# Conditioning columns from 2048 on as VectorE sums in a two-layer diffusion backbone

## What is computed

```python
silu_c = jax.nn.silu(c)
silu_cc = jax.nn.silu(c_ctx)
for l in range(DEPTH):
    mod_x = silu_c @ w_ada[l] + b_ada[l]      # 1024 x 6144 weights
    mod_c = silu_cc @ w_ada[l] + b_ada[l]
    sh1, sc1, g1, sh2, sc2, g2 = jnp.split(mod_x[:, None, :], 6, axis=-1)
    ...
    hx = _rmsnorm(x, norm1[l]) * (1.0 + sc1) + sh1
    ox, oc = _mixer(...)            # projection to 2304 columns, three kinds of heads, output projection
    x = x + g1 * ox
    hx2 = _rmsnorm(x, norm2[l]) * (1.0 + sc2) + sh2
    x = x + g2 * _ec_moe(hx2, ...)  # 16 experts, each takes its 64 best latents
    ...                             # the same for the context, in layer 0 only
return _rmsnorm(x, norm_final)
```

## Time and profile before

| | us |
|---|---|
| median of 3 runs | 1987.08 (1986.86 to 1988.47) |
| profiled execution, its own time | 1991.13 |
| its span | 1989.3 |
| TensorE busy | 1823.7 (92%) |
| VectorE busy | 658.9 (33%) |
| ScalarE busy | 365.7 (18%) |
| GpSimd busy | 225.2 (11%) |
| mean granted TensorE clock | 0.966 of full speed |

### The profile page before, as it was taken

The page is one execution under the profiler, slowest core; times in us unless marked ns, Lnnn a source line. Parts: engine busy times, 40 slices in busy tenths (PEclk is TensorE's granted clock), DMA queues, the critical chain, the costliest instruction groups (busy, mean ns, idle before and its releaser), DMA issues.

```text
span 1989.3 us, 31721 instructions
## 1 busy us (share of the span) xinstructions
PE 1823.7 (92%) x13724; PEld 938.9 (47%) x13724; DVE 658.9 (33%) x1429; ACT 365.7 (18%) x798; POOL 225.2 (11%) x303
## 2 busy tenths in 40 slices
PE   6999899999969999999999699999968999888896
PEld 3877446775424444444444488458533333222221
DVE  2422456562341111111111232676242333223233
ACT  2201334562310000000000221556220000000001
POOL 1000133000001111111111100330001000000000
PEclk7999899899979999999999799999988999999998
DMA  9247522006359999999999610000577999999995
GB/s 385 116 172 274 229 109 85 2 2 258 122 202 391 395 394 395 391 397 388 398 389 406 249 61 0 1 22 2 222 269 291 406 404 404 402 412 404 412 412 242
DMA packets 82563, 522.96 MB, mean 263 GB/s; under 512 B 11200, under 2 KB 13504, under 8 KB 23808
## 3 DMA queue, kind: packets, MB, share of 16 engines
q1 hardware_dynamic: 67104, 484.04, 60.6%
q0 software_dynamic: 13120, 36.71, 6.2%
q10 hardware_dynamic: 2208, 0.26, 0.1%
HBM read 504.19 MB, written 16.78 MB: 262 GB/s over the span
## 4 chain that ended last, share of the span: by engine, by line
PE 76%; DMA 15%; DVE 4%; ACT 3%; issue 1%; SPq 0%; POOL 0%; DVEq 0%; ACTq 0%; POOLq 0%
PE psum L1411 16%; PE psum L1405 9%; PE psum L1414 8%; PE psum L1300 7%; DMA ring<-in_w_up 7%; PE psum L1113 6%; DMA arena<-in_w_up 6%; PE psum L1073 6%; PE psum L1195 5%; PE psum L1251 2%; PE psum L1220 2%; PE psum L1169 2%; PE psum L1023 2%; PE psum L1492 2%; ACT arena L919 2%; PE psum L1153 1%
## 5 line engine op out<-in xcount | busy, mean ns | idle before, releaser
L1411 PE MATMUL psum<-ring,arena 128*32 128x512 f32 x1984 | 258.7, 593 | 1.1 <-DVE arena L1926 1.1
L1405 PE MATMUL psum<-ring,arena 128*64 128x512 f32 x976 | 228.8, 604 | 22.2 <-DMA ring<-in_w_down 12.9
L987 ACT ACTIVATE arena<-psum 128x768 f32<-128x768 f32 (+1 forms) x32 | 22.6, 705 | 941.5 <-PE psum L1414 463.4
L1414 PE MATMUL psum<-ring,arena 128*32 128x256 f32 x1984 | 152.5, 379 | 0.0
L1405 PE MATMUL psum<-arena 128*64 128x512 f32 x560 | 132.2, 607 | 16.8 <-DMA arena<-in_w_down 8.2
L1405 PEld LDWEIGHTS psum<-ring,arena 128*64 128x64 f32 x976 | 64.1, 137 | 168.0 <-issue 118.6
L1300 PE MATMUL psum<-ring,arena 128*128 128x512 f32 x320 | 142.5, 596 | 0.0
L919 ACT ACTIVATE arena<-psum,smx 128x768 f32<-128x768 f32 (+4 forms) x160 | 119.2, 750 | 109.6 <-DVE smx L1679 109.3
L1414 PEld LDWEIGHTS psum<-ring,arena 128*32 128x32 f32 x1984 | 64.5, 110 | 148.4 <-issue 148.4
L1679 DVE TENSOR_REDUCE smx<-psum 128x1 f32<-128x768 f32 (+4 forms) x160 | 115.9, 766 | 39.6 <-PE psum L1153 27.8
L708 POOL TENSOR_SCALAR arena<-arena,smx 128x768 f32<-128x768 f32 (+1 forms) x40 | 78.0, 1949 | 430.3 <-DVE smx L1744 430.3
(11 more groups left out here) (266 smaller groups left out, 2009.6 us busy)
## 6 DMA issues: line engine op xcount, KB each, us to landing
ring<-in_w_gate SPq DMA_DIRECT2D x88, 1024.0 KB, 28.1
ring<-in_w_up SPq DMA_DIRECT2D x84, 1024.0 KB, 26.9
ring<-in_w_down SPq DMA_DIRECT2D x82, 1024.0 KB, 28.1
ring<-in_w_ada SPq DMA_DIRECT2D x48, 1024.0 KB, 6.4
arena<-in_w_down SPq DMA_DIRECT2D x46, 1024.0 KB, 27.0
arena<-in_w_up SPq DMA_DIRECT2D x44, 1024.0 KB, 27.7
arena<-in_w_gate SPq DMA_DIRECT2D x40, 1024.0 KB, 28.3
ring<-in_w_in SPq DMA_DIRECT2D x18, 1024.0 KB, 23.0
```

What stands on the lines that cost most here:

```text
L1405: ins = mm(psum[64 * n:64 * n + 64, b * 512:(b + 1) * 512], lhs(k), w[:, n * 512:(n + 1) * 512], start=k == 0, stop=k == KD - 1)
L1411: ins = mm(psum[r0:r0 + 32, b * 512:(b + 1) * 512], lhs(k)[:, 32 * g:32 * g + 32], w[:, n * 512:(n + 1) * 512], start=k == 0, stop=k == KD ...
L1414: ins = mm(psum[32 * j:32 * j + 32, (b + 1) * 512:(b + 1) * 512 + 256], lhs_c(k), w[:, j * 256:(j + 1) * 256], start=k == 0, stop=k == KD - 1)
```

## The change

`w_ada` is split on the host. Columns 0 to 2047 of both layers keep their layout and their way through TensorE: four groups at the start for layer 0, and the four of layer 1 at tiles 1 to 4 of layer 0's second projection pass, one a tile (`ADA_REST`); GpSimd sends their eight units, into ring slots 8 and 10. Columns from 2048 on are laid out anew as `w_adat`, with the column on the partition and its 1024 weights in a row: 16 units a layer, each of two chunks of 128 columns. VectorE multiplies a chunk with the conditioning row, which lies on all partitions, and accumulates along the row into one column of `mod`: one `scalar_tensor_tensor` of 128x1024 a chunk and stream (`long_sums`). Its products go to a bfloat16 scratch of three rows. Layer 0 has 32 chunks by two streams, 64 sums; layer 1 has 32. The tables `LONG_A` and `LONG_D` give the number of sums at each index of the first and second pass. The units go through two ring slots that later hold the first units of the output projection, and a third slot holds the conditioning row (in layer 0 a Silu on ScalarE in place; its result is stored in DRAM and loaded again in layer 1). SP sends the row and the first two units ahead of the units of the second pass, and each other unit when the sums of the unit two before it are done. Nothing is left beside attention steps, and values always lie at column 3584.

```diff
-    ADA_REST = [(0, g) for g in range(4, 12)] + [(l, g) for l in range(1, DEPTH) for g in range(12)]
-    ADA_D = 2 * (NB + 1)
-    ADA_SLOT, ADA_SLOTS = 5, 3
-    for g in range(4):
+    ADA_REST = [(l, g) for l in range(1, DEPTH) for g in range(HEAD_GROUPS)]
+    ADA_SLOT, ADA_STRIDE, ADA_SLOTS = 8, 2, 2
+    LONG_UNITS, LONG_SLOTS = w_adat.shape[1], 2
+    LONG_CHUNK = 4 * HEAD_GROUPS
+    LONG_CHUNKS = 2 * LONG_UNITS
+    for g in range(HEAD_GROUPS):
         plan(("ada", 0, g), ada_units(0, g))
...
+    def long_slot(l, j):
+        return ring[:, (where[("wout", l)] + j) % RING, :].rearrange("p (a k) -> p a k", a=2)
+    def c_row(l, s):
+        return long_slot(l, LONG_SLOTS)[:, s, :]
+    def long_streams(l):
+        return 2 if l < DEPTH - 1 else 1
+    def long_summed(l, units):
+        return long_sum, sum(LONG_CHUNKS * long_streams(j) for j in range(l)) + 2 * units * long_streams(l)
+    LONG_A = [(0, 0, 3, 4, 4, 5, 8, 7), (0, 2, 2, 3, 3, 3, 4, 4)]
+    LONG_D = [(7, 7, 7, 6, 6, 0, 0), (3, 3, 3, 2, 0, 0, 0)]
...
     def values_at(st):
-        return 2816 if st.beside_ada else 3584
+        return 3584
...
+        def load_long_ada(l, u):
+            if u >= LONG_SLOTS:
+                sp.wait_ge(*long_summed(l, u - LONG_SLOTS + 1))
+            sp.dma_start(long_slot(l, u % LONG_SLOTS), w_adat[l, u]).then_inc(long_landed[u % LONG_SLOTS], 16)
...
-                if n == where[("wout", 0)]:
...
+                if n == where[("winD", l)]:
+                    sp.wait_ge(free, spent(where[("wout", l)] + LONG_SLOTS) - RING + 1)
+                    if l == 0:
+                        sp.dma_start(long_slot(l, LONG_SLOTS),
+                                     c_rows.rearrange("(a s) k -> a s k", a=1).broadcast_to([P, 2, D])).then_inc(s_crow, 16)
+                    else:
+                        sp.wait_ge(s_crd, 16)
+                        sp.dma_start(c_row(l, 0), silu_row.broadcast_to([P, D])).then_inc(s_crow, 16)
+                    for u in range(LONG_SLOTS):
+                        load_long_ada(l, u)
+                if n == where[("wout", l)]:
+                    for u in range(LONG_SLOTS, LONG_UNITS):
+                        load_long_ada(l, u)
+                    sp.wait_ge(*long_summed(l, LONG_UNITS))
...
+            if l == 0:
+                pool.wait_ge(s_crs, 1)
+                pool.dma_start(silu_row, c_row(0, 0)[0:1, :]).then_inc(s_crd, 16)
+                for m, (src, k) in enumerate(ada_stream):
...
+                if l == 0 and i == 1:
+                    act.wait_ge(s_crow, 16)
+                    act.activation(long_slot(0, LONG_SLOTS), long_slot(0, LONG_SLOTS), ACT.Silu).then_inc(s_crs, 1)
...
-                        if l == 0 and j:
+                        if l == 0 and 1 <= i <= len(ADA_REST):
+                            if j == 1:
+                                ada_mm(3 + i)
                             if j == 2:
-                                ada_tr(4 + 2 * i)
-                            ada_mm(4 + 2 * i + j - 1)
+                                ada_tr(3 + i)
...
-                elif l == 0:
-                    ada_mm(4 + 2 * i)
-                    ada_tr(4 + 2 * i)
-                    ada_mm(5 + 2 * i)
-                if l == 0:
-                    ada_tr(5 + 2 * i)
...
-                if ada_at(l, i - 1):
-                    ada_tr(ada_at(l, i - 1), 7)
-                if ada_at(l, i):
-                    ada_mm(ada_at(l, i), 7 * 512)
...
-                if st.kind == "D" and st.i >= 2 and steps[2 * (st.i // 2) - 1].beside_ada:
-                    pe.wait_ge(*L("mix", st.i // 2))
...
+        def long_sums(l, first, count):
+            n = long_streams(l)
+            for o in range(first, first + count):
+                c, s = divmod(o, n)
+                u, j = divmod(c, 2)
+                if o == 0:
+                    dve.wait_ge(s_crs, 1) if l == 0 else dve.wait_ge(s_crow, 32)
+                if j == 0 and s == 0:
+                    dve.wait_ge(long_landed[u % LONG_SLOTS], 16 * (l * (LONG_UNITS // LONG_SLOTS) + u // LONG_SLOTS + 1))
+                before = long_summed(l, 0)[1] + o
+                if before >= 3:
+                    dve.wait_ge(long_sum, before - 2)
+                stt(products[:, o % 3, :], long_slot(l, u % LONG_SLOTS)[:, j, :], 1.0, c_row(l, s), ALU.mult, ALU.mult,
+                    accum_out=mod[:, l, LONG_CHUNK + c, s:s + 1]).then_inc(long_sum, 1)
...
                        ).then_inc(L["rope"], 1)
+                long_sums(l, sum(LONG_A[l][:i]), LONG_A[l][i])
                 if i >= 2:
...
             for i in range(NB + 1):
-                if l == 0:
-                    for gi in (4 + 2 * i, 5 + 2 * i):
-                        ada_row(gi)
-                        ada_col(gi)
+                if l == 0 and 1 <= i <= len(ADA_REST):
+                    ada_row(3 + i)
+                    ada_col(3 + i)
                 if i < NX:
...
                     ins.then_inc(L["kde"], 1)
+                long_sums(l, sum(LONG_A[l]) + sum(LONG_D[l][:i]), LONG_D[l][i])
```

More of the change, by code:

```diff
@@ L120, in build_program @@
     convo = area(6144, 2, T)
+    products = area(6144, 3 * D // 2).bitcast(BF16).rearrange("p (a k) -> p a k", a=3)
     qT = area(BIG, 4, T)
@@ L261, in build_program @@
     ada_landed = [sem(f"ada_landed{s}") for s in range(ADA_SLOTS)]
+    long_sum = sem("long_sum")
+    long_landed = [sem(f"long_landed{s}") for s in range(LONG_SLOTS)]
+    s_crow = sem("c_rows_loaded")
+    s_crs = sem("c_rows_silu")
+    s_crd = sem("silu_row_stored")
+    s_mod = sem("mod_complete")
     free = sem("ring_free")
@@ L288, in slot @@
         return ring[:, n % RING, :].rearrange("p (k m) -> p k m", k=k)
+    def long_slot(l, j):
[8 more added lines that the diff above has]
+    LONG_D = [(7, 7, 7, 6, 6, 0, 0), (3, 3, 3, 2, 0, 0, 0)]
+    for l in range(DEPTH):
+        assert sum(LONG_A[l]) + sum(LONG_D[l]) == LONG_CHUNKS * long_streams(l)
     def arrive(e, n):
@@ L419, in conv_results @@
         return sum(ends(ks) for _, _, ks in conv_plan(l)[:max(i, 0)])
-    ADA_STEPS = (1, 3, 5, 7, 9, 11)
-    def ada_at(l, i):
-        return 4 + ADA_D + ADA_STEPS.index(i) if l == 0 and i in ADA_STEPS else None
     def reader_before(l, i):
@@ L578, in column @@
         return t[:, e:e + 1] if isinstance(e, int) else t[:, bass.ds(e, 1)]
-    ada_order = [(0, g) for g in range(4)] + ADA_REST
+    ada_order = [(0, g) for g in range(HEAD_GROUPS)] + ADA_REST
     block = es.enter_context(nc.Block())
@@ L700, in _ @@
                     pool.dma_start(ropet, rope).then_inc(L["tab"], 16)
+            if l == 0:
+                pool.wait_ge(s_crs, 1)
+                pool.dma_start(silu_row, c_row(0, 0)[0:1, :]).then_inc(s_crd, 16)
+                for m, (src, k) in enumerate(ada_stream):
+                    if m < ADA_SLOTS:
+                        pool.wait_ge(free, ADA_SLOT + ADA_STRIDE * m + 1)
+                    else:
+                        pool.wait_ge(ada_free, m - ADA_SLOTS + 1)
+                    pool.dma_start(slot(ADA_SLOT + ADA_STRIDE * (m % ADA_SLOTS), k), src).then_inc(ada_landed[m % ADA_SLOTS], 16)
             for st in ATT[l]:
@@ L1229, in values @@
                 a0 = values_at(st)
-                if l == 0 and st.i == 17:
-                    pe.wait_ge(s_col, len(ada_order))
                 if sums_here(l, st):
@@ L1563, in ada_col, with norm_scales @@
                bcol[:, l, 4 * g:4 * g + 4].unsqueeze(2).broadcast_to([P, 4, 2]), ALU.add).then_inc(s_col, 1)
-            if g in (3, 9):
-                which = 0 if g == 3 else 1
+            if g == 3:
                 dve.wait_ge(s_col, gi + 1)
-                c0 = 8 if g == 3 else 32
-                n0 = 16 + 16 * which + 8 * l
-                stt(acol[:, l, which], mod[:, l, c0:c0 + 8, :], 1.0,
-                    pack[:, n0:n0 + 8].unsqueeze(2).broadcast_to([P, 8, 2]), ALU.add, ALU.mult).then_inc(s_acol, 1)
+                norm_scales(l, 0, 2)
+        def norm_scales(l, which, n):
+            c0, n0 = (8, 32)[which], 16 + 16 * which + 8 * l
+            stt(acol[:, l, which, :, 0:n], mod[:, l, c0:c0 + 8, 0:n], 1.0,
+                pack[:, n0:n0 + 8].unsqueeze(2).broadcast_to([P, 8, n]), ALU.add, ALU.mult).then_inc(s_norm[which], 1)
+        def long_sums(l, first, count):
[12 more added lines that the diff above has]
+                    accum_out=mod[:, l, LONG_CHUNK + c, s:s + 1]).then_inc(long_sum, 1)
+            if count and first + count == LONG_CHUNKS * n:
+                dve.wait_ge(*long_summed(l, LONG_UNITS))
+                m = mod[:, l, LONG_CHUNK:, 0:n]
+                tt(m, m, bcol[:, l, LONG_CHUNK:].unsqueeze(2).broadcast_to([P, LONG_CHUNKS, n]), ALU.add).then_inc(s_mod, 1)
+                dve.wait_ge(s_mod, l + 1)
+                norm_scales(l, 1, n)
         def normed(l, t):
@@ L2039 @@
     nc = bacc.Bacc("TRN2", target_bir_lowering=False, num_devices=1)
+    ada = np.asarray(inputs["w_ada"])
```

(3 more changed lines are left out.)

42 lines of the change are left out of this document (19 added, 23 removed).

## The result

| | before | changed |
|---|---|---|
| median | 1986.97 us (1986.73 to 1988.47, 4 runs) | 1973.32 us (1969.45 to 1974.70, 4 runs) |
| profiled execution | 1991.13 | 1974.53 |
| its span | 1989.3 | 1972.6 |
| mean granted TensorE clock | 0.966 | 0.962 |

What follows compares the result with a forecast made beforehand. The chain was taken to run mostly through TensorE, with VectorE mostly idle in the projection passes. Terms -15.9 - 2.2 - 16.9 + 11.1 + 3.0 = -20.9 us gave 1966 from the median 1987.1; range 1956 to 1985.

Steps and rivals of the forecast that it cites:

- rival (b): Layer 0's second pass: clock falls in each of four stalls, awaited block at half speed; 13 us, 1979; chance 0.12.
- layer 0 up to the first scores: Layer 0's projection passes until attention's first scores: these come at 201.5 instead of 217.4, -15.9 us.
- first attention step: Layer 0, from first to next scores: 7.5 us become 5.3, as in layer 1 at full clock; -2.2.
- rest of layer 0's attention: Six conditioning groups go (13.7 us) and eight waits for VectorE's copy (3.2); -16.9.
- layer 1, first pass: End of layer 1's first projection pass: sums waiting for units delay VectorE's copies and TensorE's last transposes; +11.1 us.
- layer 1, second pass: Layer 1's second projection pass: clock is down after the preceding pause, then recovers; +3.0 us.
- The sum's cost: VectorE's accumulated 128x1024 sum, start to start: 1.22 us taken, between 1.14 and 1.48.
- Rival (a): The accumulating sum costs 1.48 us; 11.4 more in layer 0, 1.6 in layer 1, 1979; chance 0.10.
- rival (c): Accumulating sums with two float SBUF inputs run at half rate, 2.3 us each; +43, 2030, slower; chance 0.08.
- First pass of layer 0: Layer 0's first projection pass: early tiles hide their sums, TensorE's last transposes wait for VectorE's copy; +1.6 us.
- Second pass of layer 0: Layer 0's second projection pass: VectorE becomes the bound, TensorE stalls about 2.6 us a tile, 1.4 in the last.
- Rival (d): Attention is limited by exponentials or GpSimd's scaling and keeps only 7 of 17 us; 1976; chance 0.05.

Runs made afterwards that it cites:

- filled_stalls: Changed kernel with throwaway 128x256 matmuls (6, 6, 5, 3) ahead of the conditioning row's transposes in layer 0's second pass; 1963.99 us (ratio 0.9886).
- layer1_early: Changed kernel with layer 1's sums moved to early tiles of both passes, none at the end of its first pass; 1957.38 us (ratio 0.9844).
- values_shared: Changed kernel with the values of layer 0's first sixteen D steps back in the earlier PSUM place, with its wait; 1977.01 us (ratio 0.9941).
- both_filled_half: both_tables plus throwaway matmuls between second pass and first scores, four and three in layer 0, two and two in layer 1; 1944.91 us (ratio 0.9773).
- both_again: The kernel of both_tables run once more, for a second profile; 1947.00 us (ratio 0.9796).
- short_sums: Changed kernel with each sum reading 16 of its 1024 elements, loads, waits and instruction count kept; 1949.35 us (ratio 0.9805).
- again: The changed kernel measured once more, unaltered, as partner of other runs on its chip; 1970.51 us (ratio 0.9905).
- both_tables: Changed kernel, only sum tables altered: layer 0's second pass five a tile (six in last), layer 1's first pass none at its end; 1946.71 us (ratio 0.9786).

## Why the prediction came out as it did

It was right in sign and the time lies in its range, 7.3 us above the number. The range reached up to 1985 to take in rival (b), and half of rival (b) happened. By stage, forecast and found:

| term | forecast | found |
|---|---|---|
| layer 0 up to the first scores | -15.9 | -10.2 (217.4 to 207.2) |
| first attention step | -2.2 | -0.3 |
| rest of layer 0's attention | -16.9 | -19.2 |
| up to layer 1's projections | 0 | -1.4 |
| layer 1, first pass | +11.1 | +11.9 |
| layer 1, second pass | +3.0 | +2.6 |
| sum, profiled executions | -20.9 | -16.6 |

The remaining 3 us are the two profiled executions: before's lay 4.2 above its median, the changed one's 1.2.

**The sum's cost** was right at its lower end: 1.145 us start to start, not 1.22. Rival (a) falls, and rival (c) with it: the operation runs at its full rate. The Trainium skill says that this form with two non-bf16 SBUF sources halves throughput (Vector Engine (DVE) Microarchitecture Reference, Points that are easy to get wrong). That does not hold here, where both sources are float32 and the accumulator is used: 1219 ns for 1024 elements and 170 for 16 make 1.04 ns an element. The Trainium skill also says that an operation that writes out its accumulator is two instructions (VectorE: DVE Perf Modes, Two Vector instructions with no wait between them). The trace agrees: each sum has a DVE_READ_ACCUMULATOR of 82 ns behind it, and it hides beside the next sum.

**First pass of layer 0**: the forecast was +1.6. The pause is 0.4 longer (1.46 instead of 1.06), and the second pass starts at 111.4 against 111.5 before. The seventeen sums on that path are 0.075 shorter each, 1.3 in all. So this term came out 1.7 better, and the second pass up to the first scores 7.4 worse (95.8 against 88.4), which makes the 5.7 of the table's first line.

**Second pass of layer 0, the step that failed.** VectorE bounds it, the waits stand before the row transposes, at 2.98, 3.00, 2.28 and 1.38 against "about 2.6 us a tile (1.4 in the last)". What failed is the dismissal of rival (b). Its mechanism happened in three of four stalls, at about half its size: 1.6, 2.6 and 1.7 us in the blocks and 0.6 in transposes, 6.5 together where it had 13. Without it, in filled_stalls, the loops are 16.4, 15.8 and 14.9 against the forecast's 16.1, 16.1 and 14.9. That they agree so well is partly luck: with 1.145 a sum the forecast's own formula gives 15.6, 15.6 and 14.5, and a wait for a unit (0.56 in the first of them) and longer hand-overs, which it left out, fill the difference. One reason given against rival (b) was a pause of 1.06, from which nothing follows for one of 2.6; the other was a busy share of 84%, and the clock fell all the same. The same text charged a dip for the longer pause in layer 1. Whether the clock falls behind such a stall is not certain: behind the same first three stalls (2.2 to 2.95 us) the blocks took 4.85, 3.62, 5.08 in layer1_early and 5.31, 4.83, 3.62 in values_shared. So the time of this part of the program varies from run to run.

**First attention step**: the forecast let the dip at the start of attention go because layer 1 has none in the row it read. It stays (the first convolution matmuls take 5.67, not 3.70), since what precedes it stays, waits of 2.13 and 1.68 for ScalarE and VectorE; both_filled_half, with these filled, has full clock there, and its first step takes 5.25, the 5.3 of the forecast. The row in layer 1 was at full clock in the kernel before (its convolution matmuls take 2.84), but its 5.3 did not prove that: both_again has the dip there too, beside the wait for the exponential, and takes 5.33.

**Attention** gained 2.3 more than forecast. The six groups at 2.29 make 13.7; the eight waits were priced at 0.4 and are 0.53, 4.2. That is 17.9; the last 1.3 is within what this stage varies between executions (221.2 and 222.7). The eight waits belong to the changed place, as values_shared shows; the 2.29 a group was not tested by a run of its own. Step pairs of 11.9 against 12.1 forecast. Rival (d) falls.

**Layer 1** was right in mechanism and size: sums that wait for units, the last transposes held up, then the slow clock. short_sums shows that landings have the larger share, 6.7 of 11.9.

**Costed at nothing**: the Silu, its row, the output projection's weights and GpSimd's units leave no visible cost on the path: the stages there agree within 1.4. No run took them out one by one.

## What to carry to other kernels

When work moves to an idle engine, ask per stretch how much of it fits beside one tile of the busy engine, and place it by that: the same 96 sums cost some 22 to 24 us more or less by where they stand. In these kernels they cost nothing visible where they fit. An idle share over a whole pass says nothing of its last tiles, in which the busy engine has less to do. Where the other engine becomes the bound, price each stall of TensorE with what the clock may take behind it, from rows with stalls of that length. Price a dip that stands beside another engine's wait at nothing.

## What the runs showed of the hardware

- VectorE's accumulating `scalar_tensor_tensor` on two float32 inputs from SBUF costs no more than an elementwise operation of that size (1219 ns against 1224 for line 1863's); its accumulator read (82 ns) overlaps the next instruction, unlike what ScalarE's 197 ns had suggested.
- In the second pass of layer 0 the blocks behind the first three stalls (2.2 to 3.6 us) were slow in ten of twelve cases in four executions (after, again, layer1_early, values_shared), 4.83 to 6.19 us instead of 3.62. The block behind the fourth stall (1.38) never was. All four stayed at 3.62 when the stalls were filled with throwaway matmuls, in one execution, at the same DMA share.
- Executions of one kernel on one chip differ by up to 10 us (before, beside both_filled_half: 1983.5 to 1993.4). Part of such a difference shows as stretches with a lower granted clock at places without any change, as in the attentions of both_tables and both_again; 3.5 of the 8 us between those two do not.
